# A norm's last steps taken one slot earlier, each pair of chunks finished in its own slot

## The reference

```python
def rms_norm(x, g):
    y = xf * lax.rsqrt(jnp.mean(xf * xf, axis=-1, keepdims=True) + EPS)
    return (y * g).astype(x.dtype)

def ffn_sublayer(t, shift, scale, gate, g_pre, g_post, w_in, w_out):
    y = swiglu(modulate(rms_norm(t, g_pre), shift, scale), w_in, w_out)
    return t + FFN_RES * gate * rms_norm(y, g_post)
```

## The kernel before

| norm | time in the trace | beside it | groups |
|---|---|---|---|
| N1, N5, N7 | 402, 1669, 2043 us | second products of the SwiGLU (`ffn_out`), other half | 12 |
| N2, N8 | 437, 2078 us | value products `v_b`, `v_a` of the first half | 10 |
| N3 | 1295 us | output products `wo`, other half | 8 |
| N4, N6 | 1326, 1704 us | first 8 groups of the next SwiGLU (`head`), first half | 8 |

## Time and profile before

### The profile page before, as it was taken

The page is one execution under the profiler, slowest core; times in us unless marked ns, Lnnn a source line. Parts: engine busy times, 40 slices in busy tenths (PEclk is TensorE's granted clock), DMA queues, the critical chain, the costliest instruction groups (busy, mean ns, idle before and its releaser), DMA issues.

```text
span 2882.2 us, 42837 instructions
## 1 busy us (share of the span) xinstructions
PE 2770.0 (96%) x15754; PEld 2301.8 (80%) x15754; DVE 1743.8 (61%) x2907; ACT 1250.8 (43%) x2227; POOL 249.1 (9%) x342
## 2 busy tenths in 40 slices
PE   6999999999889999999999999999999899998997
PEld 4888898876656676788888898888988677878997
DVE  5677366656745444358676386773778765635764
ACT  2232355336545434445322363223553655555443
POOL 0010010111200000011000000000102120001000
PEclk8999999999999999999999999999999999999999
DMA  5555357331111121145455355553565221424654
GB/s 224 181 188 197 108 156 241 126 101 37 45 37 38 52 77 66 44 146 175 160 191 171 114 175 177 201 182 97 176 198 186 69 66 59 137 66 154 227 175 130
DMA packets 106643, 385.48 MB, mean 134 GB/s; under 512 B 12289, under 2 KB 14081, under 8 KB 104193
## 3 DMA queue, kind: packets, MB, share of 16 engines
q1 hardware_dynamic: 86370, 303.82, 32.6%
q0 software_dynamic: 20128, 79.70, 8.4%
HBM read 379.27 MB, written 4.20 MB: 133 GB/s over the span
## 4 chain that ended last, share of the span: by engine, by line
PE 85%; DVE 9%; ACT 2%; issue 2%; DMA 1%; POOL 0%; SPq 0%; DVEq 0%; POOLq 0%; ACTq 0%
PE ps L1934 23%; PE ps L1935 22%; PE ps L1942 22%; PE ps L879 3%; PE ps L917 3%; PE ps L896 3%; DVE wlo L1474 2%; PE ps L1998 1%; PE ps L2000 1%; PE ps L1995 1%; PE ps L869 1%; DVE mx L767 1%; PE ps L875 1%; DVE work L1633 1%; ACT prob L683 1%
## 5 line engine op out<-in xcount | busy, mean ns | idle before, releaser
L1474 DVE TENSOR_TENSOR wlo<-raw,whi 128x1024 fp32r<-128x1024 f32 x572 | 696.2, 1225 | 442.2 <-ACT whi L1166 441.4
L1934 PE MATMUL ps<-xhi,whi 128*128 128x512 f32 (+1 forms) x2432 | 827.2, 354 | 16.5 <-DVE xlo L1643 16.5
L1935 PE MATMUL ps<-xlo,whi 128*128 128x512 f32 (+1 forms) x2432 | 818.3, 351 | 0.0
L1166 ACT ACTIVATE whi<-raw 128x1024 fp32r<-128x1024 f32 x572 | 604.8, 1057 | 483.6 <-PE ps L1942 443.9
L1934 PEld LDWEIGHTS ps<-xhi,whi 128*128 128x128 f32 x2432 | 465.8, 192 | 85.8 <-DVE xlo L1643 18.8
L1935 PEld LDWEIGHTS ps<-xlo,whi 128*128 128x128 f32 x2432 | 466.7, 192 | 57.0
L1942 PE MATMUL ps<-xhi,wlo 128*128 128x512 f32 (+1 forms) x2432 | 507.4, 351 | 1.4 <-DVE wlo L1474 1.4
L1942 PEld LDWEIGHTS ps<-xhi,wlo 128*128 128x128 f32 x2432 | 401.8, 191 | 59.3 <-DVE wlo L1474 2.0
L1710 DVE SCALAR_TENSOR_TENSOR work<-ada,work 128x1024 f32<-128x1024 f32 x256 | 299.8, 1221 | 4.4 <-DMA ada<-in_ada_rows 4.4
L1934 PE MATMUL ps<-ghi,whi 128*128 128x256 f32 (+1 forms) x968 | 279.5, 314 | 1.9 <-ACT whi L1166 1.9
L1935 PE MATMUL ps<-glo,whi 128*128 128x256 f32 (+1 forms) x968 | 278.6, 314 | 0.0
(11 more groups left out here) (209 smaller groups left out, 3374.4 us busy)
## 6 DMA issues: line engine op xcount, KB each, us to landing
raw<-in_ffn_in SPq DMA_DIRECT2D x192, 512.0 KB, 4.8
ada<-in_ada_rows POOLq DMA_DIRECT2D x128, 512.0 KB, 4.4
raw<-in_merge SPq DMA_DIRECT2D x96, 512.0 KB, 3.7
raw<-in_ffn_out SPq DMA_DIRECT2D x88, 512.0 KB, 3.6
raw<-in_ffn_out SPq DMA_DIRECT2D x44, 384.0 KB, 3.2
raw<-in_v_a SPq DMA_DIRECT2D x32, 512.0 KB, 4.3
raw<-in_qk_a SPq DMA_DIRECT2D x32, 512.0 KB, 3.6
raw<-in_wo SPq DMA_DIRECT2D x24, 512.0 KB, 3.7
```

What stands on the lines that cost most here:

```text
L1166: act.activation(whi[:, g.ring(SPLIT), :], raw[:, g.ring(RAW), :], ACT.Copy).then_inc(hi_ready, 1)
L1474: dve.tensor_tensor(wlo[:, g.ring(SPLIT), :], raw[:, g.ring(RAW), :], whi[:, g.ring(SPLIT), :].bitcast(F32), ALU.subtract).then_inc(lo_rea ...
L1934: pe.matmul(o, w, hi[:, first + c, ph.span], start=start, stop=False)
L1935: pe.matmul(o, w, lo[:, first + c, ph.span], start=False, stop=False)
```

## The change

In `act_norm` one empty slot is taken out, so `normed_high` of chunks 0, 1 comes in slot 5 and of 6, 7 in slot 8. In `dve_norm` the `normed_low` of a pair of chunks follows the `scaled` of the same pair in the same slot, slots 5 to 8; slot 9 falls away. No instruction is added or removed.

```diff
@@ act_norm
                 inverse(HALF_STAT, ph.span, D, base(ph, "stat") + 2)
                 yield
-                yield
                 for c in range(0, KC, 2):
                     normed_high(ph, c)
                     normed_high(ph, c + 1)
@@ dve_norm
                 newton(step, dve, base(ph, "inv") + 2, HALF_STAT, ph.span, D)
                 yield
-                for c in range(0, KC + 2, 2):
-                    if c < KC:
-                        scaled(ph, c)
-                        scaled(ph, c + 1)
-                    if c:
-                        normed_low(ph, c - 2)
-                        normed_low(ph, c - 1)
+                for c in range(0, KC, 2):
+                    scaled(ph, c)
+                    scaled(ph, c + 1)
+                    normed_low(ph, c)
+                    normed_low(ph, c + 1)
                     yield
```

## The result

The changed kernel takes 2915.52 us (median of 4 executions, 2913.1 to 2917.2) against 2886.91 (4 executions, 2884.27 to 2888.2). The ratio is 1.0094, 95% interval 1.0080 to 1.0109: slower by 27 us, 23 to 31, by that ratio (the two medians are 28.6 us apart). The forecast was 2913 in a range of 2903 to 2925, with 93% for slower. The profiled execution has a span of 2908.9 us, 26.7 more than before.

The account below looks back on a forecast made before the run. TensorE, 85% of the chain, was taken to bound the kernel. Norm terms of 24.5 us plus 2.6 for the clock gave 27.1 on 2884.27, 2911.4; with the median 1.5 higher, about 2913 us, range 2903 to 2925.

Parts of the forecast that it names:

- The ring: Waits through ACT and DVE once a slot: 3.55 us against TensorE's 2.88 or 2.16; 0.42 more with an output tile.
- N1, N5, N7: Norms beside the 12 groups of `ffn_out`: TensorE late for `whi`, 4.15 us each, 12.4 us in all.
- N2, N8: Two norms, the second repeating the first: group 10 starts 3.2 us later in each, 6.4 us in all.
- N3: Norm with an output tile in every slot: TensorE waits 1.4 us for the bank; last `xlo` 1.5 us later.
- POOL's add: Follows `output_tile` and slows DVE beside it: 0 to 0.42 us more per slot with an output tile; 0.42 taken.
- N4 and N6: Norms where last `xhi`, table load and `split_hi` delay group 17: 1.6 us and 2.6 us later.
- The clock: Low-clock stretches of TensorE from new idle, none to eight more, 0 to 13.6 us; one and a half taken, 2.6.
- rival 3: The clock falls in all eight norms, one more low stretch each: 24.5 + 13.6, so 2924 us; 15%.
- 1 (an earlier end): Norm ends a slot earlier, gaining behind N3, N4, N6 at most 11.2 us: 2874.5 us; 3%.
- 2 (hidden): The later splits fall into slack, no change: 2885.7 us; 4%.
- 4 (only the short groups): Only N1, N5, N7 lose, the rest made good behind the norm: 2885.7 + 12.4 = 2898 us; 8%.
- Refills of `raw` at nothing: SP's refill waits for DVE's next `split_lo`, some 4 us late at worst, three groups loaded ahead: cost nothing.

Follow-up runs that it names:

- ACT's half alone: Against the kernel before, only ACT's empty slot taken out, DVE keeping its old order: 2910.79 against 2884.39 us, ratio 1.0096.
- the `wlo` between: The change, but from slot 5 DVE makes a pair's `scaled`, then `split_lo`, then `normed_low`; against the kernel before: 2890.9 against 2884.39 us, ratio 1.0021.
- the longer ring: The change plus two more DVE operations ahead of each pair, 0.79 us more a slot; against the kernel before: 2936.21 against 2888.36 us, ratio 1.0157.
- the last experiment: Kernel before, last group's `wlo` after the last `xlo` in N3, N4, N6: 2883.6 against 2885.14 us; with early table load in N4, N6: 2881.16, ratio 0.9988.

## Why the prediction was right, point by point

**The ring.** Forecast 3.55 us a slot, measured 3.54; with an output tile 3.97 and 4.03. That it runs through ACT's copy is shown by ACT's half alone (the whole loss), by the `wlo` between (a fifth of it left) and by the longer ring (each added 0.79 us found again, four times a norm). It is the step that carries three quarters of the sum, and it was right as a mechanism, not by number alone.

**N1, N5, N7.** 4.15 forecast, 4.25 to 4.27 measured, in waits of 0.94, 0.82, 1.22 and 0.33 us for `whi` and the slower restart behind each (forecast lateness 1.0, 1.1, 1.4, 0.7; a wait's row leaves the restart out). **N2, N8:** 3.2 forecast, 3.19 and 3.47 measured; why N8, which repeats N2 before, comes 0.28 higher is open.

**N3.** The bank is there, as forecast. PE in the trace after, to set beside the earlier trace rows:

```profile
1324.85 0.36 PE L1931 MATMUL ps<-mhi,whi 128*128 128x256 f32 x1 [1.36 <-ACT work L1282]
...
1328.83 0.38 PE L1931 MATMUL ps<-xhi,whi 128*128 128x256 f32 x1 [0.87 <-ACT work L1282]
1331.39 0.39 PE L1931 MATMUL ps<-xhi,whi 128*128 128x256 f32 x1 [1.36 <-DVE xlo L1642]
1333.73 0.58 PE L1931 MATMUL ps<-xhi,whi 128*128 128x256 f32 x1 [1.43 <-DVE xlo L1642]
```

1.36 us against the 1.4 of the working. From the `wlo` of slot 5 to the last `xlo` it takes 1320.18 to 1334.07, 13.89 us, against 11.74 before: 2.15 more, 1.5 forecast. I had POOL's add meet `split_lo` in slots 6 and 7; it met the two `scaled` there (1.35 and 1.36 us for 0.87), and those of the last pair too (1.35), which I had left out: 0.48 of the missing 0.63. The stage took 1.85 more, and 0.62 of that came back in the group behind, whose 24 matmuls took 2.88 us after and 3.50 before, when part of them ran at the low clock; the table counts this in N4.

**N4 and N6.** 1.6 and 2.6 forecast, 1.77 and 3.33 measured. That N4 comes so near is luck: without the 0.62 us that came back from N3 it is 2.39. ACT and PE behind N4, after:

```profile
1364.23 1.28 ACT L1157 ACT_TABLE_LOAD   x1
1365.53 1.06 ACT L1166 ACTIVATE whi<-raw 128x1024 fp32r<-128x1024 f32 x1
...
1365.41 1.91 PE L1939 MATMUL ps<-xhi,wlo 128*128 128x256 f32 x8
```

The chain over the table load is as forecast: from the `wlo` of slot 5 (1352.71) to the end of the last `xhi` 11.5 us, and `whi` made 13.9 behind it, 13.8 forecast. But the next group started 14.4 behind it, in N4 and in N6 alike: TensorE was still in the lo pass ahead, whose eight matmuls took 1.91 us at the low clock (1.11 at full clock, N6 in the earlier trace rows). The chain that I added up ended in the wrong place by 0.6 us. For N6 the working had TensorE at full clock, and behind N6 the granted clock now fell, which it had not before.

**The clock** is the term that was mis-sized: 2.6 us for one and a half low stretches more, in N1's kind. There the clock did not fall at all, nor in N2 and N8. The windows of PE after, in N1, behind N4 and behind N6, columns as in the earlier trace rows:

```profile
425.00:436.00 11.00, 8.63 (x68) 1.00 0.45 131
...
1359.00:1364.00 5.00, 2.56 (x16) 1.00 0.54 191
1364.00:1368.00 4.00, 3.61 (x19) 0.57 0.37 151
1742.00:1746.00 4.00, 1.94 (x12) 1.00 0.48 153
1746.00:1750.00 4.00, 3.67 (x18) 0.57 0.45 142
```

In N1 TensorE was busy 8.63 of 11 us and kept 1.00. Behind N6 it is now busy 1.94 of 4 (2.86 before) and then gets 0.57. Behind N3 the low stretch is half as long as before (3.4 us against 6.8), behind N4 it is as long (3.4), behind N6 it is new (3.4): 10.2 us at the low level in the eight norms, before and after. Nor does a low stretch always cost: in the longer ring the clock fell to 0.50 for 3.4 us in N1, after TensorE had been busy for 3.99 of 7.60 us, and not in N5 and N7; the three stages still took 7.53, 7.42 and 7.54 us more, since the ring set their pace. The Trainium skill, "TensorE: Matmul & The Clock Gate", section "What's actually happening", has activity lift the lower clock; N6 agrees with it. That all eight norms would fall to the lower clock (rival 3) does not hold: three did. That the total came so close, 27.1 us forecast and 26.7 measured in the traces, is partly luck: the terms of the norms were 1.9 us short in sum and the clock's 2.6 too long. In the working of the range, the upper end of the first span comes to 2917 and not 2918, and adding its 6 us to both ends gives 2902 and 2923 and not 2904 and 2922; the forecast does not hang on it.

**The rivals.** 1 (an earlier end) is refuted by the change in N3, N4, N6 alone; 2 (hidden) by every stage; 4 (only the short groups) by N2, N8 and by the change in N1, N5, N7 alone, 12.8 us of 26.4. Refills of `raw` at nothing: in no stage did ACT's `whi` in slots 6 to 9 wait for a DMA.

## What to carry to other kernels

When two engines hand a tile forth and back in streams ordered by hand, write down the ring: every instruction that stands between a wait and the next release, on both engines, the other work of the slot included. Compare its length with what the bounding engine takes a slot; if it is longer, the difference is paid once a slot, however idle either engine looks. The lag of one slot that the old order kept looked like an empty step and was the cover; finishing a pair "sooner" cost 1.8 to 4.3 us in each of the eight norms, and work that nobody awaits yet (here a `wlo`) is the piece to move out of the ring.

## What the runs showed of the hardware that I had not expected

**The attention stages, which no kernel here touches, differ between executions.** From the end of N2 to N3, some 650 us, the profiled execution after was 2.6 us shorter than before, the one with the `wlo` between 5.8 us longer, the two of the last experiment (`wlo` of the last group behind the norm, without and with the early table) 4.8 longer. The windows of PE there, before and with the `wlo` between:

```profile
640.00:1293.00 653.00, 623.53 (x3276) 0.99 0.18 59
```

```profile
640.00:1298.80 658.80, 629.32 (x3277) 0.98 0.18 59
```

The count of matmuls is the same but for one at the edge, and the busy time differs by as much as the stage does, at a granted clock of 0.99 and 0.98: 10.2 us at the low level in the first, 23.9 in the second. So a difference of 5 us between two profiled executions can be the clock in attention alone, and an effect of 4 us in the norms has to be read from the stages.

**A wait adds little beside the time waited.** From the end of a copy on ACT (426.60 + 0.51, N1 after) to the DVE operation that waited for it (427.14) 0.03 us passed, as in the ring of the prediction from DVE to ACT. What a wait takes away is the overlap of neighbours: the first `xlo` starts 0.18 us after `scaled` ends (426.96), where without a wait, in the kernel before, it starts 0.08 before (424.05 against 424.13).

**POOL's add slows DVE, and mostly by the same amount:** where it runs beside two `scaled` they take 1.33 to 1.40 us in the kernel before (eight pairs of nine) and 1.35 or 1.36 after, and 0.87 or 0.88 without it. The Trainium skill, "SBUF — State Buffer", section "Who interferes with whom", says that a DVE instruction with two SBUF inputs contends with a GpSimd one that reads SBUF; these rows agree.
